# Page attention of the sample group: one unit's scores in four column groups of TensorE instead of two, one set of score banks instead of two

## The reference, cut to what matters

```
def update(carry, logits, vals):
    m, l, acc = carry
    m_new = jnp.maximum(m, jnp.max(logits, axis=-1))
    corr = jnp.exp(m - m_new)
    p = jnp.exp(logits - m_new[..., None])
    l = l * corr + jnp.sum(p, axis=-1)
    acc = acc * corr[..., None] + jnp.einsum('bqhk,bkc->bqhc', p, vals.astype(jnp.float32))
    return (m_new, l, acc)

def page_step(carry, pages):
    rows = cache[layer, pages]
    logits = jnp.einsum('bqhc,bkc->bqhk', qc, rows).astype(jnp.float32) * MLA_SCALE
    return update(carry, logits, rows[..., :MLA_KV_LORA]), None
```

## Time and profile before

| | |
|---|---|
| median of 3 runs | 2269.44 us (2269.44 to 2277.1) |
| profiled execution | 2280.15 us, its span 2278.4 us |
| PE busy, PEld busy | 2109.2 us (93%), 1826.6 us (80%), 17420 instructions each |
| DVE, ACT, POOL busy | 1046.3, 524.2, 114.7 us |
| page stage | about 756 to 1008 us of the span |
| mean DMA rate | 106 GB/s over the span, 294 to 351 GB/s in most of the page stage |

### The profile page before, as it was taken

The page is one execution under the profiler, slowest core; times in us unless marked ns, Lnnn a source line. Parts: engine busy times, 40 slices in busy tenths (PEclk is TensorE's granted clock), DMA queues, the critical chain, the costliest instruction groups (busy, mean ns, idle before and its releaser), DMA issues. The chain is left out here.

```text
span 2278.4 us, 39794 instructions
## 1 busy us (share of the span) xinstructions
PE 2109.2 (93%) x17420; PEld 1826.6 (80%) x17420; DVE 1046.3 (46%) x1270; ACT 524.2 (23%) x987; POOL 114.7 (5%) x143
## 2 busy tenths in 40 slices
PE   7999967789899789979999999789999999999998
PEld 7999954565456455548898898579999999999998
DVE  5222244645688678852222434775323323422424
ACT  4000004440444233321111223342101101101111
POOL 0000000001560011110000000000000000000000
PEclk9999978779899999999999999789999999999999
DMA  6113132020796589963111130301111111111112
GB/s 207 47 46 131 33 113 84 2 61 13 249 326 251 222 308 348 348 229 137 51 37 50 45 118 10 111 19 46 48 47 47 47 47 43 49 50 40 49 57 79
DMA packets 178908, 241.70 MB, mean 106 GB/s; under 512 B 27211, under 2 KB 165427, under 8 KB 173412
## 3 DMA queue, kind: packets, MB, share of 16 engines
q1 hardware_dynamic: 172792, 155.80, 22.0%
q0 software_dynamic: 5904, 83.95, 9.9%
q10 hardware_dynamic: 92, 0.20, 0.0%
HBM read 217.20 MB, written 66.72 MB: 125 GB/s over the span
## 5 line engine op out<-in xcount | busy, mean ns | idle before, releaser
L2536 PE MATMUL ps<-xn_hi,mlp_w_hi 128*128 128x344 f32 x768 | 163.3, 321 | 2.4 <-issue 1.8
L2536 PE MATMUL ps<-u_lo,mlp_w_hi 128*128 128x344 f32 x768 | 163.0, 320 | 0.0
L2536 PE MATMUL ps<-u_hi,mlp_w_hi 128*128 128x344 f32 x768 | 162.9, 320 | 0.0
L2536 PE MATMUL ps<-mlp_xn_lo,mlp_w_hi 128*128 128x344 f32 x768 | 162.9, 320 | 0.0
L2536 PE MATMUL ps<-u_hi,mlp_w_lo 128*128 128x344 f32 x768 | 162.1, 319 | 0.0
L2536 PE MATMUL ps<-xn_hi,mlp_w_lo 128*128 128x344 f32 x768 | 162.1, 319 | 0.0
L1288 PE MATMUL ps<-mla_rt,q_now 32*32 32x256 f32 x4608 | 144.9, 384 | 12.7 <-DVE mla_rt L1381 6.5
L1381 DVE STREAM_TRANSPOSE mla_rt<-qkvT 128x1536 f32<-128x1536 f32 x72 | 124.7, 1760 | 33.4 <-DMA qkvT<-in_cache_mla,page_rows 25.6
L1699 DVE TENSOR_TENSOR hT<-hT,ps 128x1032 f32<-128x1032 f32 x28 | 34.4, 1229 | 223.9 <-PE ps L2536 223.9
L2536 PE MATMUL ps<-xn_hi,gate_w_hi 128*128 128x344 f32 x576 | 128.1, 331 | 6.3 <-DVE gate_w_lo L2047 3.4
L1288 PEld LDWEIGHTS ps<-mla_rt,q_now 32*32 32x32 f32 x4608 | 85.9, 106 | 57.2 <-issue 31.8
(11 more groups left out here) (406 smaller groups left out, 3411.0 us busy)
## 6 DMA issues: line engine op xcount, KB each, us to landing
out_s_dsa_w<-in_cache_dsa_w SPq DMA_DIRECT2D x8, 4094.0 KB, 82.1
oaT<-in_w_up SPq DMA_DIRECT2D x32, 512.0 KB, 4.1
oaT<-in_w_down SPq DMA_DIRECT2D x32, 512.0 KB, 4.2
obT<-in_w_in SPq DMA_DIRECT2D x23, 512.0 KB
gate_w<-in_w_in SPq DMA_DIRECT2D x16, 512.0 KB, 4.1
out_s_dsa_w<-in_cache_dsa_w SPq DMA_DIRECT2D x8, 1022.0 KB, 17.4
s_kv_tile<-in_cache_dsa_w SPq DMA_DIRECT2D x12, 512.0 KB, 5.3
x_scr<-qkvT SPq DMA_DIRECT2D x1, 4128.0 KB, 13.2
```

The costliest lines, as they stand in the source:

```text
L2536: last = nc.tensor.matmul(out[:, t, 0:TC], w, x[:, k, t * TC:(t + 1) * TC], start=first, stop=stop)
```

## The change

JG, the number of column groups that one unit's scores use, goes from 2 to 4. A unit's scores then take 144 calls of 128 columns instead of 72 of 256, and each call has a tile of the array of its own among sixteen. All 128 partitions of the score banks hold one unit, so there is one set of banks and not two: PE waits for the exponential of u-1 before it writes the scores of u (`at_least(pe, probs, u)`). The maximum and the exponential read 128 partitions x 512 numbers instead of 64 x 1024. The probabilities are transposed in 4 calls of 128x128 instead of 8 of 64x128. The value matmuls keep count and shape. In the merge four small copies become one, and four small fills at the stage's start go.

```diff
-JG = 2
+JG = 4
...
-        pr = sb(st, "smla_pr", [P, JN, 4, SQ])
-        half = [slice(0, JG * 32), slice(JG * 32, P)]
+        pr = sb(st, "smla_pr", [P, 2, JN, 4, SQ])
...
-                        at_least(pe, probs, u - 1)
+                        at_least(pe, probs, u)
...
-                                        ps[32 * (JG * s + g):32 * (JG * s + g) + 32, i, 0:JN * SQ], q_now[SQ * i:SQ * i + SQ, s, c, :],
+                                        ps[32 * g:32 * g + 32, i, 0:JN * SQ], q_now[SQ * i:SQ * i + SQ, s, c, :],
...
-                                        start=(c == 0), stop=(c == CB - 1), tile_position=(SQ * i, 32 * (JG * s + g)),
+                                        start=(c == 0), stop=(c == CB - 1), tile_position=(SQ * i, 32 * g),
...
-                                                   pr[half[s], n].rearrange("p i t -> p (i t)"),
-                                                   mats[half[s], C_ID + JG * 32 * s:C_ID + JG * 32 * (s + 1)])
+                                                   pr[:, s, n].rearrange("p i t -> p (i t)"), ident)
...
-                    for n in range(0, JN, 2):
-                        for g in range(4):
-                            odd, j = g // JG, g % JG
+                    for n in range(JN):
+                        for g in range(JG):
...
-                    nc.vector.tensor_reduce(acc[half[s], u % AS, KL:KL + 1], ps[half[s], 0:4, 0:JN * SQ], AX_XY, ALU.max).then_inc(own, 1)
+                    nc.vector.tensor_reduce(acc[:, u % AS, KL:KL + 1], ps[:, 0:4, 0:JN * SQ], AX_XY, ALU.max).then_inc(own, 1)
...
-                for a in range(AS):
-                    nc.vector.memset(acc[half[1 - a % 2], a, KL:KL + 2], 0.0)
```

More of the change, by code:

```diff
@@ L1307, in value @@
                     at_least(pe, acced, u - 1)
-                    for n in range(0, JN, 2):
-                        for g in range(4):
-                            odd, j = g // JG, g % JG
+                    for n in range(JN):
+                        for g in range(JG):
                             last = nc.tensor.matmul(ps[32 * g:32 * g + 32, 6 + s, 0:KL],
-                                                    pt[:, s, n + odd, 32 * j:32 * j + 32],
-                                                    rows[v][:, JN * j + n + odd, 0:KL], start=(n == 0),
-                                                    stop=(n == JN - 2), tile_position=(0, 32 * g),
+                                                    pt[:, s, n, 32 * g:32 * g + 32],
+                                                    rows[v][:, JN * g + n, 0:KL], start=(n == 0),
+                                                    stop=(n == JN - 1), tile_position=(0, 32 * g),
                                                     skip_group_check=True)
@@ L1345, in exp @@
                     at_least(act, p_turned, u - 1)
[L1346 to L1349, removed]
+                    nc.scalar.activation(pr[:, s].rearrange("p n i t -> p i n t"),
+                                         ps[:, 0:4, 0:JN * SQ].rearrange("p i (n t) -> p i n t", n=JN), ACT.Exp,
+                                         bias=negm[:, s:s + 1], scale=MLA_SCALE,
+                                         accum_out=acc[:, u % AS, KL + 1:KL + 2]).then_inc(probs, 1)
                 def copy_probs(u):
@@ L1388, in row_max @@
                     at_least(dve, stored[u % AS], 16 * (u // AS))
-                    nc.vector.tensor_reduce(acc[half[s], u % AS, KL:KL + 1], ps[half[s], 0:4, 0:JN * SQ], AX_XY, ALU.max).then_inc(own, 1)
+                    nc.vector.tensor_reduce(acc[:, u % AS, KL:KL + 1], ps[:, 0:4, 0:JN * SQ], AX_XY, ALU.max).then_inc(own, 1)
                     dve.wait_ge(own, u + 1)
-                    nc.vector.tensor_scalar(negm[half[s], s:s + 1], acc[half[s], u % AS, KL:KL + 1], -MLA_SCALE, None,
+                    nc.vector.tensor_scalar(negm[:, s:s + 1], acc[:, u % AS, KL:KL + 1], -MLA_SCALE, None,
                                             ALU.mult).then_inc(maxed, 1)
-                for a in range(AS):
-                    nc.vector.memset(acc[half[1 - a % 2], a, KL:KL + 2], 0.0)
                 for k in range(CG):
@@ L1466, in dve_weigh @@
         dve.wait_ge(part_in, 16 * (NB + 1))
[L1467 to L1471, removed]
+        last = nc.vector.tensor_copy(m[:, 0:PARTS], part[:, :, KL])
         link(last)
```

## The result

The changed kernel takes 2475.14 us (median of 4 runs, 2467.14 to 2476.03) against 2271.67 us for the one before (median of 4 runs): 1.0884 times as long, with a 95% interval of 1.0853 to 1.0915. That is 203 us slower. The forecast was 2430 us in a range of 2325 to 2545. The direction and the cause were right, and the forecast change of +161 us was a fifth too small.

The account below looks back on a forecast made before the run. Refetched instruction blocks were to bound PE: 29.7 at 7.0 us during 208 us of gathers, plus 55.3 at 3.7 us (205 us), make a stage of 413 us against 251.3. That +161 us gave 2430 us, range 2325 to 2545.

Parts of the forecast that it names:

- The instructions: PE's list in the stage: 2864 instructions before, in blocks of 251; now 648 a unit instead of 368.
- The body is fetched anew: PE's loop: the new body of 10.3 blocks is not kept, so each of seven passes fetches it.
- 85 blocks: PE's fetches in the stage: seven passes of 10.3 + 0.4 blocks make 75, with 10 before them.
- 3.7 us a block: PE's instruction fetch: cost of each block beside idle DMA engines, one after the other.
- 7.0 us beside a gather: PE's instruction fetch: cost of a block while a gather runs, set for 29.7 blocks in 208 us.
- second rival: PE's fetch runs ahead and is no bound, so the stage approaches its gathers: 2249 us, chance 4%.
- The score matmuls, 1.9 to 2.8 us a unit: PE's 288 score matmuls of a unit were to take this instead of 3.7 us, by itself gaining nothing.
- the sign that score groups would be shorter: PE in the profile after: score groups shorter than before, a check on parts that don't count.
- fourth rival: PE's matmuls can't start closer than about 25 ns, 11 us a unit: +100, 2370 us, chance 3%.
- DVE and the single set of banks: DVE's maximum saves 0.5 to 0.6 us; PE's new wait for the exponential is hidden behind blocks.
- third rival: Without a fetch bound, PE's new wait takes the gain back: 6.5 to 7 us a unit, 2265 to 2275, chance 2%.

Follow-up runs that it names:

- e3: The kernel before with PE's list written out straight for all 32 units, without its loop: 2309.73 us, ratio 1.0166.
- e2: The kernel before with each score call of 256 columns written as two of 128, layout and banks kept: 2492.21 us, ratio 1.0968.
- e1: The changed kernel with PE's loop body two units long instead of four, 5.7 blocks instead of 10.3: 2312.51 us, ratio 1.0162.
- e5: The kernel before with score calls of three blocks of latent numbers split in two, a body of 1856 instructions: 2390.49 us, ratio 1.0511.
- e6: The kernel before with score calls of five blocks of latent numbers split in two, a body of 2112 instructions: 2442.76 us, ratio 1.0726.
- e7: The changed kernel with the gathers of units 4 to 31 cut to one cache row for each partition instead of 16: 2381.47 us, ratio 1.0493.
- e10: The kernel before with score calls of two blocks of latent numbers split in two, a body of 1728 instructions: 2369.93 us, ratio 1.0438.
- e9: The kernel before with score calls of one block of latent numbers split in two, a body of 1600 instructions: 2275.35 us, ratio 1.0015.
- e8: The kernel before with a two-unit loop body and score calls of eight of nine blocks of latent numbers split in two: 2322.55 us, ratio 1.0224.

## Why the prediction was right, and where its size was off

**The instructions.** Waits at every 251st or 502nd instruction, blocks of 16 KB and the count of 2864 against 11 packets were read rightly; e3, all straight code, took the 47 blocks that the count gave.

**The body is fetched anew.** Right, as the MLP's loop had shown: q8 ran through the whole stage, 91 blocks, e2 was as slow with the old layout, and e1 took 163 of 203 us back. The limit is lower than the 8 blocks I later named for e5.

**85 blocks.** Mis-sized. I added 0.4 of a block to each pass for the branch, from the MLP. E5 and e6 fetched 69 and 77 from 745 us on. Less their straight parts (7.1 and 8.1 blocks), and over seven passes, that is 8.8 and 9.8 a pass for bodies of 7.4 and 8.4: 1.4 more. For the changed kernel that is some 7 blocks more than I had, and 91 were counted from 757 us on, 93 from 745. An extra one is seen in six of the seven passes: a packet starts 0.7 to 1.4 us behind the one before, where all others in the stage keep 3.2 us or more. Why isn't shown.

**3.7 us a block.** Nearly right: 3.8 in e7. Together with the count this is nearly the whole miss: I had 85 x 3.7 = 315 us without gathers, and e7's stage took 351, 36 us more, of which 90 blocks at 3.8 us are 27. The change in the stage was 197.6 us against 161 forecast, which is 36.6.

**7.0 us beside a gather.** Right: 29.7 slow blocks of 7.0 us were forecast, and 30 distances of 5.9 us or more, 7.2 in the mean, were found. That 29.7 x 3.3 = 98 us meets the 97.5 between e7 and the changed kernel so closely is in part luck: e7 cut 28 of the 31 gathers, for which the forecast makes 89 us. The price also rested on two distances only; pairs of blocks beside them took 5.2 and 6.1 us a block (803.50 to 813.91, 784.29 to 796.53). And the second rival's "4.5 us a block" is 4.8 by the earlier trace rows (two blocks from 803.50 to 813.11 us).

**The score matmuls, 1.9 to 2.8 us a unit.** Wrong. I read the gap from the first eight that start, which stood ready in the queue. In the long run of e1 192 took 2.73 us and 96 took 1.48, 4.2 us a unit, against 4.34 before. Half the columns on twice the tiles gained almost nothing, and the sign that score groups would be shorter failed: 192 matmuls took 3.58 us at 999.46, in part at half the granted clock, where 96 of the old ones took 2.82; at the full clock, in e1, they took 2.73. It had no effect on the forecast, since fetches cover it. The fourth rival with 25 ns was wrong as well: 13 ns were seen in e1, so the floor that the Trainium skill gives in TensorE: Matmul & The Clock Gate (about 25 ns from start to start) doesn't hold for tiles side by side.

**DVE and the single set of banks.** The maximum fell from 1.22 to 0.69 us, ACT's exponential from 1.11 to 0.69, and neither could count while PE was the bound. The new wait cost 4.9 us once. The third rival had the right mechanism for what stands behind the fetch: in e1, where blocks no longer bind, every steady unit's scores wait for the exponential. It put a unit at 6.5 to 7 us, and e1's take 176.5 / 23 = 7.7.

## What to carry to other kernels

Before splitting a matmul into more and smaller ones inside a loop, count the instructions of the body: an fp32 call is four, and here a body of 1600 on PE stayed while one of 1728 was fetched again in every pass, for 95 us. Where "issue" waits fall at a constant number of instructions, read the instruction queue by stretches: its packets show which loops are kept. Each block cost about 3.8 us here, one after the other, so code whose block runs for less than that was bound by its fetch, and most of all beside large DMAs (7.2 us). And an "issue" wait is not always a fetch: compare its end with the semaphores that the kernel itself waits for, as in e1, where it followed the exponential by 0.16 us.

## What the runs showed of the hardware that was not expected

- The limit for a kept loop body on PE lies between 6.4 and 6.9 blocks of 16 KB (1600 and 1728 instructions of matmul and weight load), and crossing it loses all of the body, not only its excess: e10 fetched 67 blocks, e9 12.
- Straight code without any branch is fetched no faster: e3 lost 36 us, and its packets are 3.4 us apart at the least.
- Beside a gather of 2.36 MB the next block starts about 7.2 us after the last one instead of 3.8 (30 such distances beside 31 gathers, 3 in e7).
- In the stream, matmuls of 32x32 tiles with 128 columns start 12 to 13 ns apart on sixteen tiles (e1) and 19 ns on eight (e8). The first 8 of the group in the earlier trace rows start within 10 ns of one another, and that pace doesn't last.
